# A fused two-block forward pass on one core: the opening's loads, first slot and TensorE activity rearranged

## The reference, cut to what matters

```python
f = swiglu(rms_norm(h, ffn_pre_g[0, 0]), ffn_w_gate[0, 0], ffn_w_up[0, 0], ffn_w_down[0, 0])
h = h + 0.5 * rms_norm(f, ffn_post_g[0, 0])

def swiglu(n, w_gate, w_up, w_down):
    return (jax.nn.silu(n @ w_gate) * (n @ w_up)) @ w_down
```

## Time and profile before

| what | value |
|---|---|
| median of three runs | 1486.06 us |
| lowest, highest | 1483.37, 1489.32 us |
| the profiled execution, its own time | 1487.02 us |
| its span, from the first to the last instruction | 1485.3 us |
| TensorE busy | 1419.8 us, 96% of the span |
| mean granted TensorE clock | 0.972 of full speed |

### The profile page before, as it was taken

The page is one execution under the profiler, slowest core; times in us unless marked ns, Lnnn a source line. Parts: engine busy times, 40 slices in busy tenths (PEclk is TensorE's granted clock), DMA queues, the critical chain, the costliest instruction groups (busy, mean ns, idle before and its releaser), DMA issues.

```text
span 1485.3 us, 19638 instructions
## 1 busy us (share of the span) xinstructions
PE 1419.8 (96%) x6476; PEld 1163.2 (78%) x6476; DVE 875.9 (59%) x1328; ACT 768.7 (52%) x1233; POOL 61.9 (4%) x92
## 2 busy tenths in 40 slices
PE   7999999898999998999999899999998899999998
PEld 6888878677888877888877678888787767788887
DVE  6655565955655556555555675555644844665554
ACT  6555466435655546555554565554655523465552
POOL 0000010500000000000010000000100100000000
PEclk9999999999999999999999999999998866999999
DMA  8767536555666544766633456665546520465661
GB/s 271 228 198 221 174 122 205 155 172 162 211 199 205 185 141 142 221 196 191 184 112 102 135 172 195 196 192 144 153 137 181 179 78 29 155 214 184 193 188 57
DMA packets 199327, 251.65 MB, mean 169 GB/s; under 512 B 19718, under 2 KB 138084, under 8 KB 199276
## 3 DMA queue, kind: packets, MB, share of 16 engines
q1 hardware_dynamic: 199152, 250.97, 53.9%
q10 hardware_dynamic: 124, 0.03, 0.0%
HBM read 249.89 MB, written 1.05 MB: 169 GB/s over the span
## 4 chain that ended last, share of the span: by engine, by line
PE 88%; DVE 5%; ACT 3%; issue 1%; DMA 1%; SPq 1%; POOL 0%; DVEq 0%; ACTq 0%
PE ps L1643 27%; PE ps L1645 27%; PE ps L1644 26%; DVE wlo L1015 3%; PE ps L1669 2%; PE ps L1755 2%; ACT whi L554 1%; DMA raw<-in_w_in 1%; PE ps L2150 1%; PE ps L2152 1%; ACT sq_out L648 1%; ACT kthi L666 0%; PE ps L1887 0%; SPq L476 0%; PE ps L2049 0%
## 5 line engine op out<-in xcount | busy, mean ns | idle before, releaser
L1015 DVE SCALAR_TENSOR_TENSOR wlo<-raw,gcol,whi 128x512 fp32r<-128x512 f32 (+1 forms) x600 | 435.9, 774 | 295.9 <-ACT whi L554 294.6
L1643 PE MATMUL ps<-whi,kthi 128*128 128x512 f32 (+2 forms) x1400 | 556.8, 398 | 26.2 <-DVE wlo L1015 14.7
L1645 PE MATMUL ps<-whi,ktlo 128*128 128x512 f32 (+2 forms) x1400 | 546.6, 390 | 0.0
L1644 PE MATMUL ps<-wlo,kthi 128*128 128x512 f32 (+2 forms) x1400 | 546.2, 390 | 0.0
L554 ACT ACTIVATE whi<-raw,gcol 128x512 fp32r<-128x512 f32 (+1 forms) x600 | 397.2, 714 | 248.3 <-PE ps L1645 223.4
L1643 PEld LDWEIGHTS ps<-whi,kthi 128*128 128x128 f32 x1400 | 267.2, 191 | 83.0 <-issue 16.8
L1645 PEld LDWEIGHTS ps<-whi,ktlo 128*128 128x128 f32 x1400 | 266.9, 191 | 55.2
L1644 PEld LDWEIGHTS ps<-wlo,kthi 128*128 128x128 f32 x1400 | 267.6, 191 | 51.0
L1023 DVE TENSOR_TENSOR wlo<-raw,whi 128x1024 fp32r<-128x1024 f32 x151 | 182.7, 1217 | 129.3 <-ACT whi L558 128.7
L558 ACT CAST whi<-raw 128x1024 fp32r<-128x1024 f32 x151 | 156.2, 1046 | 157.9 <-PE ps L1645 146.8
L1643 PE MATMUL ps<-whi,hthi 128*128 128x512 f32 x440 | 172.1, 391 | 0.0
(11 more groups left out here) (192 smaller groups left out, 737.0 us busy)
## 6 DMA issues: line engine op xcount, KB each, us to landing
raw<-in_ffn_w_gate SPq DMA_DIRECT2D x176, 256.0 KB, 2.9
raw<-in_ffn_w_up SPq DMA_DIRECT2D x176, 256.0 KB, 3.1
raw<-in_ffn_w_down SPq DMA_DIRECT2D x176, 256.0 KB, 3.4
raw<-in_w_in SPq DMA_DIRECT2D x80, 256.0 KB, 3.4
raw<-in_gmlp_w_in SPq DMA_DIRECT2D x64, 256.0 KB, 3.1
raw<-in_w_gate SPq DMA_DIRECT2D x44, 256.0 KB, 2.9
raw<-in_w_up SPq DMA_DIRECT2D x44, 256.0 KB, 3.1
raw<-in_w_down SPq DMA_DIRECT2D x44, 256.0 KB, 3.3
```

Of the source, the lines that this page charges most:

```text
L1015: ins = nc.vector.scalar_tensor_tensor(out=wlo[:, s, cut], in0=raw[:, s, cut], scalar=gcol[:, k:k + 1], in1=f32(whi[:, s, cut]), op0=ALU.m ...
L1643: nc.tensor.matmul(dst, lhs[0], rhs[0], start=first, stop=False)
L1644: nc.tensor.matmul(dst, lhs[0], rhs[1], start=False, stop=False)
L1645: return nc.tensor.matmul(dst, lhs[1], rhs[0], start=False, stop=last)
```

## The change

Nothing of the computation changes. SP issues half of token tile 0 (256 KB) first, then the early gains and slots 0 and 1; it then waits until slot 0 has landed (`raw_in[0]` at 32), and issues slots 2 and 3, token tile 1, `freq` and the positions, and slots 4 and 5 as before. ACT's queue issues `ident` and the other half of tile 0. The seven small loads of the later gains go from ACT's queue to POOL's, behind the memset of `half_neg`. Slot 0 is split by chunk on all three engines: ACT signals its first half by `first_high`, DVE by `first_low`, and TensorE's first three matmuls wait for `first_low` alone. ACT's squares of tile 0 move from ahead of `kthi` to behind slot 3's high part, tile 1's squares to behind its `kthi`. DVE's angles move from ahead of `ktlo` to behind `ffn_first`. TensorE runs matmuls on a zeroed bf16 tile (`warm`: 7 at the start, 2 behind the gains' transpose, 12 behind the flip of tile 0), into a bank that is overwritten later.

```diff
--- before.py
+++ after.py
@@ -323,9 +323,9 @@
             def chunked(w):
                 return w.rearrange("(c p) n -> p c n", p=P)
 
-            def ffn_first(w_gate, w_up):
+            def ffn_first(w_gate, w_up, slots=range(4)):
                 gate, up = chunked(w_gate), chunked(w_up)
-                for s in range(4):
+                for s in slots:
                     gate_up(s, take(s), gate, up, 0)
 
             def ffn_rest(w_gate, w_up, w_down, between=(), following=None):
@@ -380,15 +380,17 @@
                 return a["x"][0, t * P:(t + 1) * P, :]
 
 
-            sp.dma_start(ident[:], a["c_ident"]).then_inc(sem("ident_in"), 16)
+            sp.dma_start(h[:, 0, 0:BANK], tokens(0)[:, 0:BANK]).then_inc(sem("x_in0"), 16)
             r, n, ap = gain_rows[0]
             sp.dma_start(grow[r:r + n, :], ap).then_inc(sem("early_in"), 16)
+            ffn_first(a["ffn_w_gate"][0, 0], a["ffn_w_up"][0, 0], range(2))
+
+            sp.wait_ge(raw_in[0], 32)
+            ffn_first(a["ffn_w_gate"][0, 0], a["ffn_w_up"][0, 0], range(2, 4))
+            sp.dma_start(h[:, 1, :], tokens(1)).then_inc(sem("x_in1"), 16)
             sp.dma_start(freq, a["c_freq"]).then_inc(sem("pos_in"), 16)
             with nc.allow_non_contiguous_dma(reason="256 positions"):
                 sp.dma_start(pos_i[:], a["positions"][0].rearrange("(t p) -> p t", p=P)).then_inc(sem("pos_in"), 16)
-            sp.dma_start(h[:, 0, :], tokens(0)).then_inc(sem("x_in0"), 16)
-            ffn_first(a["ffn_w_gate"][0, 0], a["ffn_w_up"][0, 0])
-            sp.dma_start(h[:, 1, :], tokens(1)).then_inc(sem("x_in1"), 16)
 
             posts = [0]
 
@@ -507,6 +509,8 @@
                 pool.wait_ge(sem("pool_own"), own[0])
 
             step(nc.gpsimd.memset(half_neg[:], -0.5))
+            for r, n, ap in gain_rows[1:]:
+                pool.dma_start(grow_late[r - early_rows:r - early_rows + n, :], ap).then_inc(sem("late_in"), 16)
             for name, n, scale, eps, signals, halves in roots:
                 if name == "post_ffn000":
 
@@ -746,18 +750,26 @@
                 tile(pairs - 1, 1, then)
 
 
-            for r, n, ap in gain_rows[1:]:
-                act.dma_start(grow_late[r - early_rows:r - early_rows + n, :], ap).then_inc(sem("late_in"), 16)
-            act.wait_ge(sem("x_in0"), 16)
-            squares(h[:, 0, :], "pre_ffn000", 0, None)
+            act.dma_start(ident[:], a["c_ident"]).then_inc(sem("ident_in"), 16)
+            act.dma_start(h[:, 0, BANK:2 * BANK], a["x"][0, 0:P, BANK:2 * BANK]).then_inc(sem("x_in0b"), 16)
             flip_high(0, 6)
             flip_high(0, 7, 4)
             act.wait_ge(sem("gcol_ready"), 1)
-            highs([0, 1, 2, 3], "ffn00")
+            act.wait_ge(raw_in[0], 32)
+            k = gain_col["ffn00"]
+            nc.scalar.activation(whi[:, 0, 0:BANK], raw[:, 0, 0:BANK], ACT.Copy, scale=gcol[:, k:k + 1]
+                                 ).then_inc(sem("first_high"), 1)
+            nc.scalar.activation(whi[:, 0, BANK:UNIT], raw[:, 0, BANK:UNIT], ACT.Copy, scale=gcol[:, k + 1:k + 2]
+                                 ).then_inc(hi_done[0], 1)
+            take(0)
+            highs([1, 2, 3], "ffn00")
+            act.wait_ge(sem("x_in0"), 16)
+            act.wait_ge(sem("x_in0b"), 16)
+            squares(h[:, 0, :], "pre_ffn000", 0, None)
+            flip_high(1, 6)
+            flip_high(1, 7, 4)
             act.wait_ge(sem("x_in1"), 16)
             squares(h[:, 1, :], "pre_ffn001", 1, None)
-            flip_high(1, 6)
-            flip_high(1, 7, 4)
 
             highs([4, 5])
             ffn_first("ffn00", "pre_ffn00")
@@ -1219,10 +1231,28 @@
 
 
 
+            nc.vector.memset(sq_out[:, 1, 0:BANK], 0.0).then_inc(sem("warm_ready"), 1)
             for pair in range(2):
                 nc.vector.memset(st(f"free{pair}"), 0.0).then_inc(sem("wide_read"), 1)
             dve.wait_ge(sem("gcol_full"), 1)
             nc.vector.tensor_copy(gcol[:, 0:early_rows], ps[:, 5, 0:early_rows]).then_inc(sem("gcol_ready"), 1)
+
+            flip_low(0, 6)
+            flip_low(0, 7, 4)
+            dve.wait_ge(sem("first_high"), 1)
+            k = gain_col["ffn00"]
+            for c, done in enumerate((sem("first_low"), lo_done[0])):
+                if c:
+                    dve.wait_ge(hi_done[0], take(0) + 1)
+                cut = slice(c * BANK, (c + 1) * BANK)
+                nc.vector.scalar_tensor_tensor(out=wlo[:, 0, cut], in0=raw[:, 0, cut], scalar=gcol[:, k + c:k + c + 1],
+                                               in1=f32(whi[:, 0, cut]), op0=ALU.mult, op1=ALU.subtract).then_inc(done, 1)
+            lows([1, 2, 3], "ffn00")
+            flip_low(1, 6)
+            flip_low(1, 7, 4)
+
+            lows([4, 5])
+            ffn_first("ffn00", "pre_ffn00")
 
             dve.wait_ge(sem("pos_in"), 32)
             mark(nc.vector.tensor_copy(posf, pos_i[:]))
@@ -1245,14 +1275,6 @@
                 mark(nc.vector.tensor_scalar(dst, dst, quarter * 2.0 * math.pi, PI_DOWN, ALU.add, ALU.min))
                 settle()
                 nc.vector.tensor_scalar(dst, dst, -PI_DOWN, None, ALU.max).then_inc(sem("ang_ready"), 1)
-            flip_low(0, 6)
-            flip_low(0, 7, 4)
-            lows([0, 1, 2, 3], "ffn00")
-            flip_low(1, 6)
-            flip_low(1, 7, 4)
-
-            lows([4, 5])
-            ffn_first("ffn00", "pre_ffn00")
 
             dve.wait_ge(sem("gcol_full"), 2)
             nc.vector.tensor_copy(gcol[:, early_rows:row], ps[:, 7, 0:row - early_rows]).then_inc(sem("gcol_ready"), 1)
@@ -1684,6 +1706,8 @@
                         pe.wait_ge(sem("h_new"), 4 * (k - 1) + 2 * t + b + 1)
                     elif b == 0:
                         pe.wait_ge(sem(f"x_in{t}"), 16)
+                    elif t == 0:
+                        pe.wait_ge(sem("x_in0b"), 16)
                 flip(t, lambda c, t: h[:, t, c * P:(c + 1) * P], ready=renewed)
 
             def tile_product(n_of, bank=4):
@@ -1703,7 +1727,10 @@
                 base = seen["kt_ready"] - 2
                 for t in range(TT):
                     for s in range(4):
-                        made(s, n_of(s))
+                        if k or t or s:
+                            made(s, n_of(s))
+                        else:
+                            pe.wait_ge(sem("first_low"), 1)
                         if s % 2 == 0:
 
                             pe.wait_ge(sem("kt_ready"), base + 2 * t + s // 2 + 1)
@@ -1712,6 +1739,8 @@
                             flip_h(k, 1)
                         for c in range(2):
                             kc = 2 * s + c
+                            if k == t == s == 0 and c:
+                                made(0, n_of(0))
                             rhs = slot(s, lambda x: x[:, c * BANK:c * BANK + width])
                             ins = product(ps[:, 4 + t, 0:width], kt(kc, t), rhs, kc == 0, kc == KC - 1)
                         if t:
@@ -1855,12 +1884,20 @@
                 count("wide_read", 2 * pairs)
 
 
+            def warm(n):
+
+                for _ in range(n):
+                    nc.tensor.matmul(ps[:, 0, :], sq_out[:, 1, 0:P], sq_out[:, 1, 0:BANK], start=True, stop=True)
+
+            pe.wait_ge(sem("warm_ready"), 1)
+            warm(7)
             pe.wait_ge(sem("ident_in"), 16)
             pe.wait_ge(sem("early_in"), 16)
             nc.tensor.transpose(ps[:, 5, 0:early_rows], grow[0:early_rows, :], ident[0:early_rows, 0:early_rows]
                                 ).then_inc(sem("gcol_full"), 1)
+            warm(2)
             flip_h(0, 0)
-
+            warm(12)
             pe.wait_ge(sem("gcol_ready"), 1)
             ffn_first(0)
```

## The result

The changed kernel is slower: 1488.64 us (median of 20 runs, 1483.54 to 1492.26) against 1484.36 us for the kernel before beside it (20 runs, 1483.18 to 1489.72), a ratio of 1.0022 with a 95% interval of 1.0013 to 1.0032. That is within the half per cent that the forecast called "same", but on the other side of 1: a gain of 2.0 us was forecast, a loss of about 3 us (1.9 to 4.7 by the interval) came, and 1488.64 lies above the range, which ended at 1488.4. The profiled execution took 1489.85 us.

A forecast was written before the change was run, and what follows sets the result against it. TensorE bounds the kernel, busy 1419.8 of 1485.3 us, so only the opening can gain. First product 2.7 us earlier, low level's 1.8 gone, waits 1.0 and 0.8 new, 0.7 given back: net 2.0, 1486.06 to 1484.1 us, range 1480.3 to 1488.4.

The forecast's parts named there:

- First product: Opening, TensorE: the first product starts at 9.1 us instead of 11.76, 2.7 us earlier.
- Tile 1's wait: Opening: token tile 1 lands at 13.7 us, TensorE wants it at 12.9 and stands 0.8 us.
- the 0.7 us to be given back in the next block: `gate_up(1, 0)`: slot 3 ready at about 28.0 us, wanted at 27.4; 0.7 of the 2.7 us lost, 2.0 left.
- The second limit: Next block: ACT's row of work has slot 3 ready at about 28.0 us, putting `hid_flip(0)` at 29.4 instead of 31.38.
- The recorded signs of being wrong: Products at 0.43 us, `h<-in_x` wait beyond 1 us, wait before line 1869, `htlo` releasing `down(0)`, attention low-clock spell of another length.
- Warming and the flip: Opening, TensorE: clock rises at about 5.0 us, tile 0's flip is over at about 6.3, at the latest 7.4.
- POOL and the angles: POOL's seven issues at 1.2 us each, over at 9.5; DVE's angles end at 32.3, cover 1.3 us: both cost nothing.
- Behind it TensorE is full, and the rest moves as a block.: Everything after the opening and next block: the net 2.0 us gain carries unchanged to the end.
- a different pattern of low-clock spells in the attention, which I see no cause for: Rival: more than 0.5% (7.4 us) faster, needing other low-clock spells in the attention; chance 0.03.
- the clock stays low until the warm block's end: Rival, opening: flip to 7.4 us, first product at 12.5; only 1.2 us won, 1484.9; chance 0.2.
- Tile 1 was late: Rival: nothing is won; tile 1 lands at 16.4 us rather than 13.7, time 1486.1; chance 0.1.
- POOL's issues: Rival: slower; POOL's issues delay `late_in`, loss over 7.4 us only at 4.3 us an issue, some 1494; chance 0.04.

The follow-up runs named there:

- e4: The changed kernel once more, nothing altered, timed beside the kernel before: 1487.65 us, ratio 1.0016.
- e11: The changed kernel, POOL keeping its seven small loads, with seven more copies of them on ACT's queue into spare space: 1484.41 us, ratio 0.9993.
- e14: The changed kernel, small loads on POOL, with seven one-column copies on ACT in place of the loads: 1484.3 us, ratio 0.9996.
- e15: The changed kernel with the seven small loads back on ACT's queue, measured once more: 1484.66 us, ratio 1.0011.
- e7: The changed kernel with the seven small loads back on ACT's queue, nothing on POOL's: 1484.0 us, ratio 0.9997.
- e12: The changed kernel with the small loads back on ACT and discarded 256-column matmuls in twelve of TensorE's stage-boundary pauses: 1488.59 us, ratio 1.0013.
- e18: The changed kernel with DVE's low parts of slots 2 and 3 moved later in layer 1's first feed-forward: 1491.34 us, ratio 1.0027.
- e1: The changed kernel with 8 discarded matmuls (1.8 us) on TensorE ahead of the late gains' transpose: 1490.05 us, ratio 1.0025.
- e5: The changed kernel without any of its 21 warm matmuls: 1487.52 us, ratio 1.0011.
- e8: The kernel before with its seven small late-gain loads moved to POOL's queue, nothing else changed: 1486.75 us, ratio 1.0019.
- e10: The kernel before with ACT's seven small loads moved to SP's queue behind token tile 1, nothing on POOL's: 1489.4 us, ratio 1.0014.
- e6: The kernel before with only the 21 warm matmuls added: 1484.05 us, ratio 0.9992.
- e9: The kernel before, ACT keeping its seven small loads, with seven copies of them on POOL's queue into spare space: 1484.98 us, ratio 1.0008.
- e13: The kernel before with one small 128x128 copy added on ACT between the high parts at 758 us: 1483.91 us, ratio 1.0006.
- e16: The kernel before with one unused 128x128 reduction on DVE, lengthening TensorE's stop at 762 us: 1485.08 us, ratio 0.9999.
- e17: The kernel before with DVE's low parts of slots 2 and 3 moved later in layer 1's first feed-forward: 1491.2 us, ratio 1.0029.

## Why the prediction was wrong

*The opening, step by step.* Right in kind in the changed kernel's own profile. First product 8.49 (forecast 9.1), wait for slot 1 0.84 (1.0), line 1869 at 23.68 (near 23), `gate_up(1, 0)` 23.88, `hid_flip(0)` 29.53 (29.4), `down(0)` without a wait.

Two terms of the sum were mis-sized, and they nearly cancel. Tile 1's wait is 1.81 for 0.8: the tile was issued at 8.73 and took 5.62 us, landing at 14.36 where 13.7 was taken, so that 1.75 us are won at the late gains' transpose and not 2.7. And the 0.7 us to be given back in the next block were not: its slot 3 was ready at 27.99, as forecast (28.0), but TensorE came to it 1 us later than forecast and hardly had to wait, and 1.69 of the 1.75 were left. The second limit was right, so the total hardly shows the first miss. The recorded signs of being wrong include a wait on `h<-in_x` beyond 1 us and a spell of another length in the attention; both came. Warming and the flip were better than taken, since the level had risen by the flip (eight transposes from 5.19 to 6.06, 0.87, as in the earlier trace rows). Net 1.7 us won of the 2.0 forecast, in this execution. The other profiles of the new opening have the transpose 0.9 to 1.4 us ahead of the middle of the old ones (25.4) in e4, e11, e14 and e15, and 0.7 to 1.4 us behind it in e7, e12 and e18, where tile 1 kept TensorE waiting for 2.35 us or more and the clock fell (in e1 the wait was as long and it did not fall). A gain of 1.7 us as a property of the kernel isn't shown.

*POOL and the angles.* Both costed at nothing, and right as far as their own queues go. The first and the last of POOL's seven issues, with the end of the wait for the angles on ACT:

```profile
1.35 0.75 POOL L513 DMA_DIRECT2D arena<-in_mix_pre_g  x1 [0.43 <-POOL half_neg L511]
...
4.59 0.52 POOL L513 DMA_DIRECT2D arena<-in_gmlp_b_s  x1
```

```profile
32.21 0.26 ACT L778 ACTIVATE rcos<-arena 128x64 f32<-128x64 f32 x1 [5.99 <-DVE arena L1277]
...
32.52 0.56 ACT L606 CAST hthi<-ps 128x512 fp32r<-128x512 f32 x1
```

An issue on POOL takes 0.50 to 0.75 us where 1.2 was taken, and 3.3 to 4.4 us pass until these loads of 1 to 8 KB land. A load of 16 KB on SP's queue in the same microseconds landed after 3.2, so that POOL's came 0.1 to 1.2 us later. The Trainium skill (DMA: Bandwidth & Descriptors, Latency and other measured facts) gives about 1 us to the first byte on the software path and about 0.6 on the hardware path; no row here shows a first byte, and these landings don't contradict it.

*The step that failed* is the one sentence behind the sum: "Behind it TensorE is full, and the rest moves as a block." It doesn't move as a block. In the profile of before TensorE stops 36 times behind the opening for 0.9 to 3 us from start to start, and once, for a load, for 6.3; and whether the next 3 to 10 us run at half speed is not settled by the work alone: it differs from run to run, and from kernel to kernel. The forecast had the case by name, "a different pattern of low-clock spells in the attention, which I see no cause for", but gave it 0.03, only for faster, and only in the attention. It came as slower, and in the profile its larger part in layer 1's mixer.

*The cause that wasn't seen* is in the diff's plainest line. The seven loads were costed on the queue that gained them. Nothing was asked of the engine that lost them, since ACT had time to spare. In five kernels whose ACT program is shorter ahead of the feed-forwards and that bear no padding (the changed kernel, e4, e5, e8, e10) the ratios are 1.0022, 1.0016, 1.0011, 1.0019 and 1.0014, mean 1.0016. In the eight where ACT has all its instructions (e6, e7, e9, e11, e13, e14, e15, e16) they are 0.9992, 0.9997, 1.0008, 0.9993, 1.0006, 0.9996, 1.0011 and 0.9999, mean 1.0000. Some of each have the new opening, some the old: the opening doesn't sort them, ACT's length does. By the quotients of medians the five are 1.0018 to 1.0029 and the eight 0.9990 to 1.0002, with no overlap. The loss goes with the clock: beside before, the mean granted clock is 0.0011 to 0.0019 lower in e4, e5, e8 and e10, and 0.0005 lower on average in the eight. So the thirteen together show that the shorter ACT program goes with the loss, and the swaps in both directions (e8, and e7, e11 and e14) make it the cause; most single intervals are too wide to say so by themselves, and the first kernels had suggested the grouping. It is not the only way to such a loss, nor is the full program a guard: e17 has it and is at 1.0029 by an edit on DVE, and e12, at 1.0013, has it beside its fills. Lengths other than these few were not tried.

*What stays open.* How seven instructions less cost 2 to 3 us is not settled. Shown are ACT's stop of 0.32 to 0.43 us ahead of or within that row of high parts, DVE's and TensorE's stop behind it longer by 0.21 to 0.27 us at 762, and, in the changed kernel, e1, e4 and e5, one at 844 to 853 us of 2.31 in place of 2.02. Not shown is that these are what lowers the clock: e16 has TensorE's longer stop at 762 and isn't slow, and e8 and e10 are without the second. They may act together, or through stops too short to be told apart here. Open too, in part, is where the opening's gain goes in e7, e11, e14 and e15, which have it and ACT's full length: 0.9997, 0.9993, 0.9996 and 1.0011, mean 0.9999, where a gain of 1.7 us would make 0.9989. Their profiled openings end 1.4, 1.3 and 0.9 us earlier than the old ones and once 0.7 later, which is less than 1.7. And by the mean clock of all their runs, at 1.2 us for 0.001, an estimate gives them spans 1.1 to 1.6 us shorter than before's at an equal clock, with a clock up to 0.0016 lower that takes most of it back. e15's interval does not hold 0.9989 by itself; the other three hold both.

*The rivals.* That the clock stays low until the warm block's end did not come true: tile 0's flip ran at the high level in the changed kernel's profile, and so did the products. The Trainium skill (TensorE: Matmul & The Clock Gate, Part 4), by which transposes count less than matmuls, neither gains nor loses by it: this flip lasted 0.87 us between matmuls. Tile 1 was late, in this profile by 0.7 us and not 2.7; in e18, where its flip starts at 16.26, it was nearly as late as that rival had it. POOL's issues were far from harm.

## What to carry to other kernels

Where an instruction is taken off an engine's program, ask what follows it there too, even if the engine is idle half the time: seven copies that do nothing, put where the loads had been, gave back the 0.2% that the seven loads' move had cost. A kernel bound by TensorE with many short stops between stages has a spread of its own (here 1481.5 to 1495 us in e13 alone) that goes with the clock, so judge a gain of a few microseconds by ratios over a dozen runs, and look at the clock's column of each window before believing a profile. That holds for the place of the edit itself: the opening's 1.7 us were read from one profile, and the next one of the same kernel (e4) has 0.9. An edit that moves a stop by a microsecond can cost several, though the sum of stops is the same.

## What the runs showed of the hardware

- TensorE's clock fell to its lower level after stops as short as 0.66 and 0.83 us between stretches of full work (the changed kernel at 202 us), and stops of 0.62 and 0.83 us at the same place in before were not followed by such a fall. Spells differ between executions of one program: the changed kernel's profile has them at 202, 786 and 800 us, e4's, of the same kernel, has not. A mean granted clock lower by 0.001 goes with about 1.2 us of a span of 1485.
- ACT stops for 0.32 to 0.43 us in a row of high parts where it has nothing to wait for that the profile shows (e10: 0.32 `<-issue`), at a place that moves with the number of instructions ahead of it. A transfer of the trace's instruction queue `q14` moves too, and begins 0.6 to 1.7 us after that stop is over.
- Filling TensorE's stops by discarded matmuls gained nothing in time (e12: 1.0013, interval 0.9996 to 1.0031).
- The same load of token tile 1, 512 KB, took 5.4 to 6.6 us from issue to landing in the profiles of the new opening, and the stop that waits for `w_in` lasted 3.4 to 7.3 us.
